# Second block's attention: probabilities and values in high and low float32r parts, three products for one float32 product

## The reference, cut to what matters

```python
def attend_2(q_nope, q_rope, k_nope, k_rope, v):
    s = (jnp.einsum("bqhd,bkhd->bhqk", q_nope, k_nope)
         + jnp.einsum("bqhr,bkr->bhqk", q_rope, k_rope)) * ATTN_SCALE
    p = jax.nn.softmax(s.astype(jnp.float32), axis=-1).astype(v.dtype)
    return jnp.einsum("bhqk,bkhd->bqhd", p, v)
```

## Time and profile before

| | |
|---|---|
| median of three runs | 5525.56 us (5514.93 to 5533.5) |
| the profiled execution's own time | 5525.75 us |
| its span | 5524.0 us |
| PE busy | 4350.9 us (79%) |
| DVE busy | 2888.4 us (52%) |
| ACT busy | 1861.8 us (34%) |
| POOL busy | 617.6 us (11%) |
| granted TensorE clock, mean | 0.859 |
| this attention stage | 2997 to 3783 us of the span |

### The profile page before, as it was taken

The page is one execution under the profiler, slowest core; times in us unless marked ns, Lnnn a source line. Parts: engine busy times, 40 slices in busy tenths (PEclk is TensorE's granted clock), DMA queues, the critical chain, the costliest instruction groups (busy, mean ns, idle before and its releaser), DMA issues. The chain is left out here.

```text
span 5524.0 us, 56250 instructions
## 1 busy us (share of the span) xinstructions
PE 4350.9 (79%) x21480; PEld 3270.0 (59%) x21480; DVE 2888.4 (52%) x4273; ACT 1861.8 (34%) x3198; POOL 617.6 (11%) x858
## 2 busy tenths in 40 slices
PE   6758868678885984647876999998673868899998
PEld 4644557566664563536662565555562657688777
DVE  3454456564545545565553445443555755466545
ACT  3322342323432243232341333332322434334333
POOL 0001012210000101120001121210003600011100
PEclk7968887779897996767897999999786979999999
DMA  4000013213400000000411000002100044211134
GB/s 146 16 19 0 8 66 131 81 66 118 143 16 19 1 19 16 8 5 24 141 33 31 4 4 7 4 1 92 46 1 2 1 156 149 69 55 52 46 130 145
DMA packets 173532, 285.88 MB, mean 52 GB/s; under 512 B 43402, under 2 KB 98698, under 8 KB 173268
## 3 DMA queue, kind: packets, MB, share of 16 engines
q1 hardware_dynamic: 172516, 282.07, 15.2%
q0 software_dynamic: 608, 0.08, 0.1%
q10 hardware_dynamic: 144, 0.15, 0.0%
HBM read 257.01 MB, written 25.26 MB: 51 GB/s over the span
## 5 line engine op out<-in xcount | busy, mean ns | idle before, releaser
L307 DVE TENSOR_TENSOR x_low<-buf_a,x_high 128x1280 fp32r<-128x1280 f32 (+4 forms) x336 | 358.2, 1066 | 652.6 <-ACT x_high L290 651.7
L290 ACT CAST x_high<-buf_a 128x1280 fp32r<-128x1280 f32 (+4 forms) x336 | 310.0, 923 | 746.2 <-PE ps L330 627.1
L328 PE MATMUL ps<-x_high,w_high 128*128 128x256 f32 (+1 forms) x1344 | 498.0, 371 | 80.2 <-DVE w_low L311 78.3
L941 ACT ACTIVATE pt<-ps 128x512 f32<-128x512 f32 (+1 forms) x488 | 289.6, 594 | 745.6 <-PE ps L884 744.0
L894 PE MATMUL ps<-pt,v 128*128 128x512 f32 (+1 forms) x976 | 505.2, 600 | 0.0
L329 PE MATMUL ps<-x_low,w_high 128*128 128x256 f32 (+1 forms) x1344 | 492.0, 366 | 0.0
L330 PE MATMUL ps<-x_high,w_low 128*128 128x256 f32 (+1 forms) x1344 | 488.0, 363 | 0.0
L965 DVE TENSOR_REDUCE mx<-ps 128x1 f32<-128x1280 f32 (+1 forms) x200 | 289.8, 1449 | 343.2 <-PE ps L851 341.7
L3027 PE MATMUL ps<-w_high,x_high 128*128 128x512 f32 x896 | 370.0, 413 | 110.2 <-DVE w_low L2900 65.1
L3028 PE MATMUL ps<-w_low,x_high 128*128 128x512 f32 x896 | 363.3, 405 | 0.0
L3029 PE MATMUL ps<-w_high,x_low 128*128 128x512 f32 x896 | 362.4, 404 | 0.0
(11 more groups left out here) (388 smaller groups left out, 8816.2 us busy)
## 6 DMA issues: line engine op xcount, KB each, us to landing
w<-in_w_out SPq DMA_DIRECT2D x26, 2048.0 KB, 7.9
w<-in_w_mod SPq DMA_DIRECT2D x24, 2048.0 KB, 8.2
w<-in_w_down SPq DMA_DIRECT2D x15, 2048.0 KB, 7.8
w<-in_w_in SPq DMA_DIRECT2D x12, 2048.0 KB, 10.4
w<-in_w_up SPq DMA_DIRECT2D x22, 1024.0 KB, 7.6
w<-in_w_in SPq DMA_DIRECT2D x16, 1024.0 KB, 5.0
x<-in_x SPq DMA_DIRECT2D x16, 512.0 KB, 3.5
scratch_x<-x SPq DMA_DIRECT2D x16, 512.0 KB, 5.3
```

The costliest lines, as they stand in the source:

```text
L290: act.copy(xh[i % NX][:, 0:s["tn"]], x_of(s)).then_inc(x_high, 1)
L307: dve.tensor_tensor(xl[i % NX][:, 0:s["tn"]], x_of(s), xh[i % NX][:, 0:s["tn"]].bitcast(F32), ALU.subtract).then_inc(x_low, 1)
L328: pe.matmul(g["out"], lhs[0][:, :], rhs[0][:, :], start=(s["kk"] == 0), stop=False)
L941: act.activation(pt[g % NPT][:, 0:w["nq"]], ps[:, 4 + g % 2, 0:w["nq"]], ACT.Exp, scale=scale).then_inc(exped, 1)
```

## The change

The stage gets a function of its own, `latent_attention`; `attention` stays for the first block. What it does differently:

- `pv` becomes three float32r products: high values by high probabilities, low values by high probabilities, high values by low probabilities. It runs **three** steps behind the scores, not two (`LAG = 3`).
- ACT, after each exponential, also copies it into a rounded tile `probs_high`; POOL subtracts that from the exponential into `probs_low`. There are two tiles for exponentials (`NPT`, in `kr_t`'s memory) and four each for the high and low parts (`NPR`). The exponential of step g waits for `probs_low` of step g-2.
- The high parts of keys and queries are made by ACT, after the first exponential of the unit; the low parts stay on POOL, queries after the first `probs_low` of a unit, keys in two halves after the second and the fourth.
- Values are kept in high and low parts; ACT copies them to `v_raw` and to the high tile (three copies for two), POOL subtracts (`values_low`). The next evacuation of values waits for that.
- The projection groups lie after steps 0, 1, 3, 5 and 7 of unit 4p+2 (groups 0 to 4) and after steps 1, 3 and 5 of unit 4p+3 (groups 5 to 7).
- `qr` lies in the upper half of the tile `attn_t`, which gives room for the new tiles.

```diff
 # PairProjections.evacuate, values
-            act.copy(V[:, t0:t0 + n, 0:HD], src[:, :, 0:HD])
-            act.copy(V[:, t0:t0 + n, 2 * HD:3 * HD], src[:, :, HD:2 * HD]).then_inc(self.out, 1)
+            if p or g > 5:
+                act.wait_ge(self.v_low, 3 * p + g - 5)
+            else:
+                act.wait_ge(self.rows_set, 1)
+            act.copy(self.v_raw[:, 0:n, :], src)
+            act.copy(vh[:, t0:t0 + n, 0:HD], src[:, :, 0:HD])
+            act.copy(vh[:, t0:t0 + n, 2 * HD:3 * HD], src[:, :, HD:2 * HD]).then_inc(self.out, 1)
+
+    def values_low(self, pool, p, g):
...
+        pool.wait_ge(self.out, 8 * p + g + 1)
+        for a, b in ((0, 0), (HD, 2 * HD)):
+            ins = pool.tensor_tensor(vl[:, t0:t0 + n, b:b + HD], self.v_raw[:, 0:n, a:a + HD],
+                                     vh[:, t0:t0 + n, b:b + HD].bitcast(F32), ALU.subtract)
+        ins.then_inc(self.v_low, 1)
...
 # PairProjections.constant_rows
-        for v in V:
-            dve.memset(v[:, :, HD:2 * HD], 1.0)
+        dve.memset(v_raw[:, 0, 0:HD], 1.0)
+        dve.memset(v_raw[:, 1, 0:HD], 0.0).then_inc(self.v_high, 1)
+        dve.wait_ge(self.v_high, 1)
+        for high, low in V:
+            dve.tensor_copy(high[:, :, HD:2 * HD], v_raw[:, 0:1, 0:HD].to_broadcast([P, NT, HD]))
+            dve.tensor_copy(low[:, :, HD:2 * HD], v_raw[:, 1:2, 0:HD].to_broadcast([P, NT, HD]))
...
+def latent_attention(k, units, lay, scale, pairs):
+    NPT, NPR, LAG = 2, 4, 3
...
+            at = {0: 0, 1: 1, 3: 2, 5: 3, 7: 4} if u % 4 == 2 else {1: 5, 3: 6, 5: 7}
...
+            # POOL
+            for g in range(5, 8):
+                pairs.values_low(pool, 0, g)
+            pairs.place_rope(pool, 0)
+            keys_low(0, 0)
+            keys_low(0, 1)
+            queries_low(0)
+            for u in range(U):
+                for i in range(KEYS):
+                    g = KEYS * u + i
+                    pool.wait_ge(probs_high, g + 1)
+                    if g >= NPR:
+                        pool.wait_ge(pv_done, g - NPR + 1)
+                    pool.tensor_tensor(prl[g % NPR][:, :], pt[g % NPT], prh[g % NPR][:, :].bitcast(F32),
+                                       ALU.subtract).then_inc(probs_low, 1)
+                    pool.wait_ge(probs_low, g + 1)
+                    if u + 1 < U:
+                        if i == 0:
+                            queries_low(u + 1)
+                        if u % 2 and i in (1, 3):
+                            keys_low((u + 1) // 2, i // 2)
+                    p = u // 4 + 1
+                    if p < pairs.n and u % 4 == 2 and i == 8:
+                        pairs.place_rope(pool, p)
+                    if p < pairs.n and u % 4 == 3 and i in (2, 4, 6):
+                        pairs.values_low(pool, p, 4 + i // 2)
...
+            # PE
+            def pv(u, i):
...
+                pe.wait_ge(probs_low, g + 1)
+                vh, vl = units[u]["v"](i)
+                o = ps[:, 6 + u % 2, :]
+                pe.matmul(o, vh, prh[g % NPR][:, :], start=(i == 0), stop=False)
+                pe.matmul(o, vl, prh[g % NPR][:, :], start=False, stop=False)
+                pe.matmul(o, vh, prl[g % NPR][:, :], start=False, stop=(i == KEYS - 1)).then_inc(pv_done, 1)
...
+                    scores(u, i)
+                    if i >= LAG:
+                        pv(u, i - LAG)
+                    elif u >= 1:
+                        pv(u - 1, KEYS - LAG + i)
+                    if u + 1 < U:
+                        if i in (2, 4, 6, 7):
+                            row_scores(u + 1, (2, 4, 6, 7).index(i))
+                        if i == 8:
+                            turn(u + 1)
...
+            # ACT, ahead of unit 0: the eight evacuations, keys_high(0), queries_high(0)
+                    act.wait_ge(st_ready, g + 1)
+                    if g >= NPT:
+                        act.wait_ge(probs_low, g - NPT + 1)
+                    act.activation(pt[g % NPT], ps[:, 4 + g % 2, :], ACT.Exp, scale=scale).then_inc(exped, 1)
+                    if g >= NPR:
+                        act.wait_ge(pv_done, g - NPR + 1)
+                    act.wait_ge(exped, g + 1)
+                    act.copy(prh[g % NPR][:, :], pt[g % NPT]).then_inc(probs_high, 1)
+                    if i == 0 and u + 1 < U:
+                        queries_high(u + 1)
+                        if u % 2:
+                            keys_high((u + 1) // 2)
...
 # second_block
-    qr = lay("qr", [P, 4, LAT])
+    qr = attnT[:, 4:8, :]
...
-    V = [lay("v0", [P, NT, 3 * HD]), room("v1", [P, NT, 3 * HD])]
+    V = [[lay(f"v_{n}{i}", [P, NT, 3 * HD], F32R) for n in ("high", "low")] for i in range(2)]
+    v_raw = lay("v_raw", [P, 4, P])
...
-    attention(k, units, room, room, 96 ** -0.5, False, pairs)
+    latent_attention(k, units, Rooms(room, lay), 96 ** -0.5, pairs)
```

More of the change, by code:

```diff
@@ L1648, with __init__, uses @@
 class PairProjections:
-    def __init__(self, k, n, cqT, ckvT, krT, qr, Q, Kt, V, wts):
+    def __init__(self, k, n, cqT, ckvT, krT, qr, Q, Kt, V, v_raw, wts):
         self.k, self.n = k, n
         self.cqT, self.ckvT, self.krT, self.qr, self.Q, self.Kt, self.V, self.wts = cqT, ckvT, krT, qr, Q, Kt, V, wts
+        self.v_raw = v_raw
         self.sems = k.sems("pair_weights_in0", "pair_weights_in1", "pair_products", "pair_out", "rope_placed",
-                           "rows_zeroed", "rows_set")
+                           "rows_zeroed", "rows_set", "values_high", "values_low")
         self.w_in = self.sems[0:2]
-        self.ready, self.out, self.placed, self.zeroed, self.rows_set = self.sems[2:]
-    def uses(self, pv_done, q_low, k_low, pv_before):
-        self.pv_done, self.q_low, self.k_low, self.pv_before = pv_done, q_low, k_low, pv_before
+        self.ready, self.out, self.placed, self.zeroed, self.rows_set, self.v_high, self.v_low = self.sems[2:]
+    def uses(self, pv_done, q_high, q_low, k_high, k_low, pv_before):
+        self.pv_done, self.q_high, self.q_low, self.k_high, self.k_low = pv_done, q_high, q_low, k_high, k_low
+        self.pv_before = pv_before
     def load(self, sp):
@@ L1697, in evacuate @@
     def evacuate(self, act, p, g):
-        ps, Q, Kt, V = self.k.ps, self.Q, self.Kt, self.V[p % 2]
+        ps, Q, Kt, vh = self.k.ps, self.Q, self.Kt, self.V[p % 2][0]
         act.wait_ge(self.ready, 8 * p + g + 1)
@@ L1702, in evacuate @@
             if g == 0 and p:
+                act.wait_ge(self.k_high, 2 * p)
                 act.wait_ge(self.k_low, 2 * p)
@@ L1708, in evacuate @@
             if g == 3 and p:
+                act.wait_ge(self.q_high, 4 * p)
                 act.wait_ge(self.q_low, 4 * p)
@@ L1717, in evacuate @@
             src = ps[:, 3, 0:n * P].rearrange("p (t e) -> p t e", t=n)
-            act.copy(V[:, t0:t0 + n, 0:HD], src[:, :, 0:HD])
-            act.copy(V[:, t0:t0 + n, 2 * HD:3 * HD], src[:, :, HD:2 * HD]).then_inc(self.out, 1)
+            if p or g > 5:
[6 more added lines that the diff above has]
+    def values_low(self, pool, p, g):
+        t0 = 4 * (g - 5)
+        n = min(4, NT - t0)
+        vh, vl = self.V[p % 2]
+        if p == 0 and g == 5:
+            pool.wait_ge(self.rows_set, 1)
+        pool.wait_ge(self.out, 8 * p + g + 1)
[3 more added lines that the diff above has]
+        ins.then_inc(self.v_low, 1)
+        pool.wait_ge(self.v_low, 3 * p + g - 4)
     def wait_bank(self, pe, u):
         p = u // 4
-        issued = 8 * (p + 1) + (4 if u % 4 == 3 and p + 1 < self.n else 0)
+        issued = 8 * (p + 1) + (5 if u % 4 == 3 and p + 1 < self.n else 0)
         pe.wait_ge(self.out, issued)
@@ L1730, in wait_values, with wait_keys, wait_queries @@
         pe.wait_ge(self.out, 8 * (p + 1))
-    def wait_keys(self, pool, p):
+        pe.wait_ge(self.v_low, 3 * (p + 1))
+    def wait_keys(self, engine, p):
         if p == 0:
-            pool.wait_ge(self.rows_set, 1)
-        pool.wait_ge(self.out, 8 * p + 3)
+            engine.wait_ge(self.rows_set, 1)
+        engine.wait_ge(self.out, 8 * p + 3)
+    def wait_queries(self, engine, p):
+        engine.wait_ge(self.placed, p + 1)
+        engine.wait_ge(self.out, 8 * p + 5)
     def place_rope(self, pool, p):
@@ L1740, in place_rope @@
         if p:
+            pool.wait_ge(self.q_high, 4 * p)
             pool.wait_ge(self.q_low, 4 * p)
-        pool.wait_ge(self.k_low, 2 * p + 1)
         pool.tensor_copy(Q[0][64:96, :], qr[32 * (h % 4):32 * (h % 4) + 32, h // 4, :])
@@ L1745, in place_rope @@
         pool.wait_ge(self.placed, p + 1)
-        pool.wait_ge(self.out, 8 * p + 5)
     def constant_rows(self, dve):
@@ L1754, in constant_rows @@
         dve.memset(Kt[0][96:97, :], 1.0)
-        for v in V:
-            dve.memset(v[:, :, HD:2 * HD], 1.0)
+        v_raw = self.v_raw
+        dve.memset(v_raw[:, 0, 0:HD], 1.0)
[4 more added lines that the diff above has]
+            dve.tensor_copy(low[:, :, HD:2 * HD], v_raw[:, 1:2, 0:HD].to_broadcast([P, NT, HD]))
```

(9 more changed lines are left out.)

178 lines of the change are left out of this document (added).

## The result

The changed kernel takes **5554.9 us** (median of seven runs, 5550.07 to 5567.66); the kernel before, run beside it on the same chip, 5529.69 us (seven runs, 5514.93 to 5538.83). The ratio is 1.0049, with a 95% interval of 1.0035 to 1.0063: slower by half a per cent, or 25.2 us (19 to 35 by the interval). The forecast was 5556, which is 30 us above the kernel before, with 0.60 on slower.

What follows compares the result with a forecast made beforehand. PE was taken to set the pace, with a chain over DVE almost as long. Terms of 12.8 - 6 - 2 - 0.5 + 8 = +12.3, plus 18 for the clock, made +30 on 5525.75: 5556 us, range 5520 to 5590.

Steps and rivals of the forecast that it cites:

- The step: PE's step falls from 1.56 to 1.40 us through the three-product pv; 51 us over 320 steps if nothing else were late.
- The chain: Last pv, DVE's reciprocal and first maximum, second row scores: 16 units without projections each 0.8 us longer, +12.8 us.
- Units with projections: Units 4p+2 take 28.6 us (+2.1), units 4p+3 take 23.7 (-3.0); seven pairs of them, -6 us.
- The start: Ahead of the first unit, extra copies, subtractions and later high keys and queries delay the first scores, +8 us.
- The clock: PE's new 2.4 us pause lowers its clock in two of three of the 16 units without projections, +18 us.
- The number: Whole kernel: +30 us on the profiled execution's 5525.75 us, giving 5556 us; 0.60 on slower.
- ACT and POOL: Their new casts and subtractions per step, 1.3 and 1.35 us, fit under the 1.40 us step; taken as nothing.
- B: Rival: DVE's chain lengthens units as forecast but PE's clock does not fall; 5538 us, chance 0.24.
- A: Rival: DVE's chain is shorter than forecast, so PE's saving of 51 us less 8 comes through; 5483 us, chance 0.13.
- C: Rival: POOL sets the pace, by longer hand-offs or a queue in unit 4p+3 that doesn't drain; 5586 us, chance 0.13.
- PE's busy share of the stage: Sign to be seen in the profile: PE's share of the stage falls from nearly all to 80 to 85%.

Runs made afterwards that it cites:

- late_early_dve: late_early with the subtractions for low queries and low keys moved from POOL to DVE; 5485.42 us, ratio 0.9917 to the kernel before.
- before_late_norm: The kernel before, with DVE normalising a unit one unit later in the second block only; 5517.89 us, ratio 0.9982.
- late_norm: The changed kernel with DVE normalising a unit one unit later, so no maximum waits behind the reciprocal; 5499.74 us, ratio 0.9952 to the kernel before.
- before_lag3: The kernel before, with its float32 pv three steps behind the scores instead of two in the second block only; 5582.29 us, ratio 1.0100.
- late_early: late_norm with ACT's and POOL's work ahead of the first unit reordered to make high keys and queries earlier; 5501.26 us, ratio 0.9943 to the kernel before.
- filled_pause: The changed kernel with ten unread float32r products in PE's pause before the second row scores, units without projections; 5538.15 us, ratio 1.0020 to the kernel before.
- lag2: The changed kernel with pv two steps behind the scores instead of three; 5544.62 us, ratio 1.0022 to the kernel before.

## Why the prediction was right, step by step

**The step.** 1.40 was forecast and 1.38 to 1.40 is there, 0.16 to 0.18 less than before. The 51 us that this is over 320 steps don't arrive in after. With what is late next taken away, late_early_dve ends 45 us under before; but some 9 of these are waits that the kernel before could lose as well (before_late_norm). Against that kernel the stage is 34 us shorter, two thirds of the 51.

**The chain.** Reciprocal at 4.48 forecast, 4.42 measured; 5.66 to the row scores, exact; unit at full clock 21.16, measured 21.05 to 21.07. Over 16 units +11.0 for +12.8: the term was 0.1 us a unit too large, 0.06 of it from three steps taken at 1.40 each that measure 1.38 to 1.40. late_norm takes the chain away and before_lag3 lengthens it alone; both did what it says.

**Units with projections.** 28.6 and 23.7 forecast, 28.55 and 23.71 measured. In total -6.0 for -6. These were sums over shapes read in the earlier trace rows, and that a displayed end is modelled (1.95 for 1.72) mattered.

**The start.** +8 forecast, +7.6 measured, closer than the 2 us by which starts differ can show: the first row scores come 6.4 us later from the stage's start (6.8), and 1.2 more pass until the first score (1.2), with a granted clock of 0.50 all the way, for 0.65 before. late_early showed that it is the order of ACT's and POOL's lists.

**The clock.** +18 forecast, +23.9 in the profiled run and 16 by the medians of after and filled_pause. Thirteen of 16 units fell, not two in three; a fall cost 1.55 us and not 1.7, and in three units, with the longer low stretch, 2.9. The term held in part by luck: in the profiled run it was 6 us too small, and it is only over many runs that fewer falls bring it near 18. The bounds from two single pauses in four were the weakest term, and the range leaned on them. By the rule that the Trainium skill states in "TensorE: Matmul & The Clock Gate" (psum-queue depth-cycling), as the prediction read it, every unit would fall; 5, 9 and 20 didn't, behind a pause of the same length, so the trace agrees with it in direction and not in number.

**The number.** 5556 against 5554.9 flatters the forecast. It said 30 us over before, and 25.2 came (34.4 in the stage of the profiled runs); the rest is that before's own median was 5525.56 when the forecast was made and 5529.69 beside after. The mechanism is borne out piece by piece by the table, the agreement within 1 us is luck.

**ACT and POOL.** Both were taken as nothing, which holds for after: 2.0 us of waits for low probabilities. It holds only because PE pauses 2.3 us for DVE anyway. Take that pause away and POOL costs 1.1 us in every unit 4p+1 (late_norm) and 2.6 with less lag (lag2: 22.28 against 19.7 in 4p). The 0.12 us between 1.28 and a step of 1.40 was the right thing to distrust.

**The rivals.** B, the chain without the clock at 5538, is the filled_pause kernel, 5538.15; that the two agree within 0.2 us is luck, since before's own medians are 5525.56 to 5530.58. A asked for a first maximum before 9.3 us of a unit; in after it ends at 10.0 (3255.16 + 1.49 - 3246.63), so A was out. Its price, 5483, is about what late_early_dve reaches, by other orders on three engines. C, POOL, isn't seen in after, and is the bound of late_norm and lag2. Of what was to be seen in the profile one thing was wrong: PE's busy share of the stage was to be 80 to 85% and is 92% (700 of 758 us). It was 99% before. I had taken the share of the plain units (18.25 of 21.05 is 87%) and not counted that units with projections stay at 96 to 97%, nor that low clock is busy time too. No term of the sum used it.

**What stays open.** Why 13 of 16 nearly equal pauses lower the clock and three don't, and why three of the 13 low stretches are twice as long. And the seven runs of after spread over 18 us, of which the profile can split only its own.

## What to carry to other kernels

Work taken off the busiest engine pays only up to the next chain. Ask which instruction of the other engines is waited for, and by how much a new lag moves what it hangs on: here three short steps in place of two long ones put a reciprocal 1.0 us later and turned a gain of 51 us into a loss. A short pause of TensorE has a price of its own beyond its length. Where an in-order queue has a slow instruction that nobody is in a hurry for (3.35 us of reciprocal ahead of a maximum), put it behind the ones that somebody waits for; this small edit was worth 57 us of the changed stage and 9 of the old.

## What the runs showed of the hardware

Pauses of 2.15 to 2.38 us inside an otherwise full stretch of products lowered TensorE's granted clock to 1.2 GHz in 13 of 16 units (after), pauses of 2.0 us in 11 of 16 (before_lag3), and pauses of 0.44 us in none (before). A fall cost 1.3 to 1.7 us, in three units of after 2.9; with ten unread products in the pause there was none (filled_pause). Length alone doesn't decide: units 5, 9 and 20 of after kept 2.4 GHz, and in lag2 one of eight units with waits up to 1.35 us lost it. At the full clock a float32 product of 128x512 held TensorE for 0.86 us and a float32r one for 0.23. DVE and POOL hold each other up in subtractions from SBUF: on POOL 1.29 us became 2.43 and 0.735 became 1.86, on DVE 1.48 became 1.99. A subtraction of 128x512 took 0.69 us on DVE and 1.28 on POOL; "GPSIMD Engine Reference" in the Trainium skill (section 4.1) puts GpSimd at about twice VectorE's time, and the trace agrees. Low queries and low keys together were better placed on DVE, by 11.5 us of stage, even with what the two engines take from each other; no run moves the queries alone.
